# Rotating the second layer's queries and keys inside the projections, and summing the modulation with the ones as the stationary operand

## The reference

```python
mod_l = (silu(c) @ w_mod[l] + b_mod[l])
mod_c = (silu(c_ctx) @ w_mod[l] + b_mod[l])
```

```python
x1, x2 = x[..., :half], x[..., half:]
rotated = concatenate([x1 * cos - x2 * sin, x2 * cos + x1 * sin])
o = attend(qn, rotate(qr), kn, rotate(kr), v)
```

## Time and profile before

| | |
|---|---|
| Runs of the kernel before | 2794.28, 2802.24, 2805.22 us (median 2802.24) |
| The profiled execution | 2797.42 us, of which the span of its instructions is 2795.4 us |
| TensorE busy | 2476.6 us (89% of the span) |
| VectorE busy | 1182.4 us (42%) |
| ScalarE busy | 422.6 us (15%) |
| GpSimd busy | 856.1 us (31%) |
| Mean granted TensorE clock | 0.938 of full speed |

### The profile page before, as it was taken

The page is one execution under the profiler, slowest core; times in us unless marked ns, Lnnn a source line. Parts: engine busy times, 40 slices in busy tenths (PEclk is TensorE's granted clock), DMA queues, the critical chain, the costliest instruction groups (busy, mean ns, idle before and its releaser), DMA issues. The chain is left out here.

```text
span 2795.4 us, 30212 instructions
## 1 busy us (share of the span) xinstructions
PE 2476.6 (89%) x8861; PEld 1129.2 (40%) x8862; DVE 1182.4 (42%) x2415; ACT 422.6 (15%) x891; POOL 856.1 (31%) x1012
## 2 busy tenths in 40 slices
PE   6999887693799999999995997997399999999995
PEld 2565344441333333333332643554233333333332
DVE  2998364635523233332349213322632332323227
ACT  2000145020000000000013212322000000000002
POOL 0111102110454545545413001001255455454532
PEclk8999878796899999999997999998699999999997
DMA  6757001102699999999965300101589999999857
GB/s 247 231 196 241 20 1 61 51 30 84 242 368 368 354 353 355 356 365 359 365 260 223 94 31 9 61 23 41 202 310 345 337 330 338 336 335 335 332 209 278
DMA packets 164013, 634.28 MB, mean 227 GB/s; under 512 B 51710, under 2 KB 58282, under 8 KB 113634
## 3 DMA queue, kind: packets, MB, share of 16 engines
q10 hardware_dynamic: 59984, 389.57, 37.6%
q0 software_dynamic: 55280, 129.67, 12.8%
q1 hardware_dynamic: 48676, 114.13, 11.0%
HBM read 609.96 MB, written 74.58 MB: 245 GB/s over the span
## 5 line engine op out<-in xcount | busy, mean ns | idle before, releaser
L1813 POOL DMA_INDIRECT xg<-rows_x,p_idx x520 | 529.3, 1018 | 232.2 <-issue 124.6
L1901 PE MATMUL p_gu<-ring,p_xT 128*128 128x512 f32 x1024 | 455.8, 599 | 26.3 <-DVE p_xT L2142 26.3
L1913 PE MATMUL p_gu<-ring,p_xT 128*64 x1024 | 453.2, 595 | 0.0
L1914 PE MATMUL p_gu<-ring,p_xT 128*64 128x512 f32 x1024 | 453.1, 595 | 0.0
L2148 DVE TENSOR_TENSOR p_hid<-p_gu,p_sg 128x256 f32<-128x256 f32 x128 | 54.4, 425 | 580.6 <-ACT p_sg L2026 580.6
L1901 PEld LDWEIGHTS p_gu<-ring,p_xT 128*128 128x128 f32 x1024 | 192.0, 193 | 244.4 <-issue 244.4
L2142 DVE STREAM_TRANSPOSE p_xT<-xg 128x1024 f32<-128x1024 f32 x130 | 263.7, 2028 | 28.8 <-DMA xg<-rows_x,p_idx 27.1
L2158 DVE COPY p_ys<-p_y 128x512 f32<-128x512 f32 x128 | 88.5, 692 | 365.8 <-PE p_y L1942 187.8
L1913 PEld LDWEIGHTS p_gu<-ring,p_xT 128*64 128x64 f32 x1024 | 135.0, 137 | 263.9 <-issue 256.2
L1940 PE MATMUL p_y<-ring,p_hT 128*64 x512 | 233.4, 598 | 5.1 <-issue 5.1
L1929 PE MATMUL p_y<-ring,p_hT 128*128 128x512 f32 x512 | 236.8, 605 | 0.0
(11 more groups left out here) (450 smaller groups left out, 2975.7 us busy)
## 6 DMA issues: line engine op xcount, KB each, us to landing
ring<-in_w_exp_gate ACTq DMA_DIRECT2D x120, 1024.0 KB
ring<-in_w_exp_up ACTq DMA_DIRECT2D x120, 1024.0 KB
ring<-in_w_exp_down ACTq DMA_DIRECT2D x120, 1024.0 KB
ring<-rows_y SPq DMA_DIRECT2D x80, 512.0 KB, 13.0
decays<-in_w_mod POOLq DMA_DIRECT2D x24, 1024.0 KB
cat_e<-in_w_mod POOLq DMA_DIRECT2D x16, 1024.0 KB, 6.2
xg<-rows_x,p_idx POOLq DMA_INDIRECT x520
p_wmod<-in_w_mod SPq DMA_DIRECT2D x4, 2048.0 KB, 19.7
```

The costliest lines, as they stand in the source:

```text
L1813: nc.gpsimd.indirect_dma_start(out=xg[q][:, part * D // QUADS:(part + 1) * D // QUADS], out_offset=None, in_=tr.rows_x[:, :].rearrange("t ...
L1901: mm = nc.tensor.matmul(gu[q][:], xT[q][:, k, :], w[:, :, k, :], start=(k == 0), stop=(k == KD - 1))
L1913: nc.tensor.matmul(gu[q][lower, :], xT[q][:, k, lower], wa[:, :, k, :], start=first, stop=last)
L1914: mm = nc.tensor.matmul(gu[q][upper, :], xT[q][:, k, upper], wb[:, :, k, :], start=first, stop=last)
```

## The change

The rotation's phase goes. `latent_up` gets its work: the two loads on SyncE behind the load of `wk`, a tile's swap product on TensorE behind jobs 12, 17, 22, 27 and 32 (`krT` first), the product with the sines on VectorE one job later, the cosines on GpSimd, and the sum on VectorE ahead of jobs 16, 21, 26, 31 and 36. Two of the eight banks are given to the swap products.

In `even_project` the column of ones becomes the stationary operand and the item's buffer of 256 columns the moving one, so an item takes one matmul that writes one row of 256 numbers, at partition 0 or 64 of one of two banks. TensorE waits once, for the last item of the pair, and issues both products. ScalarE copies each row to SBUF, behind its drain of the job, and SyncE stores each row with a transfer of its own (64 in all, 1 KB each). The transpose and VectorE's two copies go.

```diff
@@ even_project
-        mcols, mturn = ph.ps("mcols", [P, P]), ph.ps("mturn", [P, P])
+        rows = spare[:, 4:6, :].rearrange("p t (a n) -> p (t a) n", n=MC)
+        sums = [ph.ps(f"sums{i}", [P, 512]) for i in range(2)]
             @block.sync
-                sp.wait_ge(mod_rows, 1)
-                for layer, s, ms in runs:
-                    r, lo = column[ms[0]], slices[items[ms[0]][0]][1] * MC
-                    sp.dma_start(tr.mod_raw[layer, s, lo:lo + len(ms) * MC].rearrange("(r c) -> r c", c=P),
-                                 mrows[r:r + HALVES * len(ms), :]).then_inc(stored, 16)
-                sp.wait_ge(stored, 16 * len(runs))
+                for m, (i, s) in enumerate(items):
+                    layer, n = slices[i]
+                    sp.wait_ge(copied, m + 1)
+                    sp.dma_start(tr.mod_raw[layer, s:s + 1, n * MC:(n + 1) * MC],
+                                 rows[m % 2 * SUB:m % 2 * SUB + 1, m // 2 % ROWS, :]).then_inc(stored[m // 2 % ROWS], 16)
+                for q in range(ROWS):
+                    sp.wait_ge(stored[q], 16 * sum(m // 2 % ROWS == q for m in range(len(items))))
             @block.tensor
                     for m in in_slot[n - 1] if n else []:
-                        pe.wait_ge(part_done, m + 1)
-                        for i in range(HALVES):
-                            mm = nc.tensor.matmul(mcols[:, column[m] + i:column[m] + i + 1],
-                                                  part[m % ABUF][:, i * P:(i + 1) * P], tr.ones[:, 0:1],
-                                                  start=True, stop=True)
-                        mm.then_inc(reduced, 1)
-                    if n == slots + 1:
-                        pe.wait_ge(copied, 1)
-                        nc.tensor.transpose(mturn[:], columns, tr.ident[:]).then_inc(mod_turned, 1)
+                        pe.wait_ge(part_done, in_slot[n - 1][-1] + 1)
+                        if m >= 4:
+                            pe.wait_ge(copied, m - 3)
+                        at = m % 2 * SUB
+                        nc.tensor.matmul(sums[m // 2 % 2][at:at + 1, 0:MC], tr.ones[:, 0:1], part[m % ABUF][:],
+                                         start=True, stop=True).then_inc(reduced, 1)
             @block.vector
-                    if n == slots + 1:
-                        dve.wait_ge(reduced, len(items))
-                        nc.vector.tensor_copy(columns, mcols[:]).then_inc(copied, 1)
-                        dve.wait_ge(mod_turned, 1)
-                        nc.vector.tensor_copy(mrows, mturn[:]).then_inc(mod_rows, 1)
             @block.scalar
+                    for m in in_slot[n - 1] if n else []:
+                        act.wait_ge(reduced, m + 1)
+                        q, at = m // 2 % ROWS, m % 2 * SUB
+                        if m >= 2 * ROWS:
+                            act.wait_ge(stored[q], 32 * (m // (2 * ROWS)))
+                        nc.scalar.copy(rows[at:at + 1, q, :], sums[m // 2 % 2][at:at + 1, 0:MC]).then_inc(copied, 1)
@@ latent_up
-    NB = 8
+    NB = 6
+    FIRST, APART = MH + MH // 2, 5
+    rotating = [krT[:, NCTX:T]] + [qrT[:, i, :] for i in range(MH // 2)]
             @block.sync
+                sp.dma_start(swap[:], dr["c_swap"]).then_inc(rope_loaded, 16)
+                sp.dma_start(rope[:], dr["c_rope"]).then_inc(rope_loaded, 16)
+            @block.gpsimd
+            def _(pool):
+                pool.wait_ge(rope_loaded, 32)
+                for n, x in enumerate(rotating):
+                    pool.wait_ge(swapped, n + 1)
+                    nc.gpsimd.tensor_tensor(x, x, rope[:, 0, :], ALU.mult).then_inc(cosines, 1)
             @block.tensor
+                def swap_halves(n):
+                    if n == 0:
+                        pe.wait_ge(rope_loaded, 32)
+                    else:
+                        at = jobs.index(("qr", n - 1, 0))
+                        pe.wait_ge(read_dve if engines[at] == "dve" else read_act, drains.count(at + 1, engines[at]))
+                    if n >= 2:
+                        pe.wait_ge(sines, n - 1)
+                    nc.tensor.matmul(swaps[n % 2][:], swap[:], rotating[n], start=True, stop=True).then_inc(swapped, 1)
...
+                    if n >= FIRST and (n - FIRST) % APART == 0 and (n - FIRST) // APART < len(rotating):
+                        swap_halves((n - FIRST) // APART)
             @block.vector
+                    if n > FIRST and (n - FIRST) % APART == 1 and (n - FIRST) // APART < len(rotating):
+                        turn_halves((n - FIRST) // APART)
+                    if n > FIRST and (n - FIRST) % APART == 4 and (n - FIRST) // APART < len(rotating):
+                        add_cosines((n - FIRST) // APART)
@@ odd_mixer
-                rotate(tr, [qrT[:, i, :] for i in range(MH // 2)] + [krT[:, NCTX:T]])
```

More of the change, by code:

```diff
@@ L375, in even_project @@
     in_slot = [[m for m in range(len(items)) if m // 2 * slots // (len(items) // 2) == n] for n in range(len(jobs))]
[L376 to L379, removed]
+    ROWS = 8
     loads = [1, 1, 1 + 2 * SKV + 1, 2, 1 + 2 * SKV + 1 + 1]
@@ L388, in even_project @@
         part = [ph.sb(f"part{i}", [P, MC]) for i in range(ABUF)]
-        columns, mrows = (spare[:, 4, i * P:(i + 1) * P] for i in range(2))
-        mcols, mturn = ph.ps("mcols", [P, P]), ph.ps("mturn", [P, P])
+        rows = spare[:, 4:6, :].rearrange("p t (a n) -> p (t a) n", n=MC)
+        sums = [ph.ps(f"sums{i}", [P, 512]) for i in range(2)]
         wm_loaded = [ph.sem(f"wm_loaded{i}") for i in range(MBUF)]
         term, part_done, reduced = ph.sem("term"), ph.sem("part_done"), ph.sem("reduced")
-        copied, mod_turned, mod_rows = ph.sem("mod_copied"), ph.sem("mod_turned"), ph.sem("mod_rows")
-        stored = ph.sem("mod_stored")
+        copied, stored = ph.sem("mod_copied"), [ph.sem(f"mod_stored{i}") for i in range(ROWS)]
         def target(kind, i, x):
@@ L717, in _ @@
                         .then_inc(gated, 1)
[L720 to L764, removed]
 def local_attention(tr, sqT, skT, sv, cat, qkT, aT, qa, kb, carry):
@@ L2401, in _, with latent_up @@
                 place(NT - 1)
-def latent_up(tr, cqT, ckvT, qnT, qrT, knT, v, wn, wr, q_loaded):
+def latent_up(tr, cqT, ckvT, qnT, qrT, knT, krT, v, wn, wr, q_loaded):
     nc, dr = tr.nc, tr.dram
@@ L2418, in latent_up @@
         bank = [ph.ps(f"bank{i}", [P, 512]) for i in range(NB)]
+        rope, swap, part = ph.sb("rope", [P, 2, NLAT]), ph.sb("swap", [P, P]), ph.sb("part", [P, 2, NLAT])
+        swaps = [ph.ps(f"swaps{i}", [P, NLAT]) for i in range(2)]
+        rope_loaded, swapped, sines = ph.sem("rope_loaded"), ph.sem("swapped"), ph.sem("sines")
+        cosines, rotated = ph.sem("cosines"), ph.sem("rotated")
         kv_loaded, product = ph.sem("kv_loaded"), ph.sem("product")
@@ L2459, in _, with turn_halves, add_cosines @@
                     mm.then_inc(product, 1)
+                    if n >= FIRST and (n - FIRST) % APART == 0 and (n - FIRST) // APART < len(rotating):
+                        swap_halves((n - FIRST) // APART)
             @block.vector
             def _(dve):
+                def turn_halves(n):
+                    dve.wait_ge(rope_loaded, 32)
+                    dve.wait_ge(swapped, n + 1)
+                    nc.vector.tensor_tensor(part[:, n % 2, :], swaps[n % 2][:], rope[:, 1, :], ALU.mult).then_inc(sines, 1)
+                def add_cosines(n):
+                    x = rotating[n]
+                    dve.wait_ge(sines, n + 1)
+                    dve.wait_ge(cosines, n + 1)
+                    nc.vector.tensor_tensor(x, x, part[:, n % 2, :], ALU.add).then_inc(rotated, 1)
                 for n, job in enumerate(jobs):
+                    if n > FIRST and (n - FIRST) % APART == 1 and (n - FIRST) // APART < len(rotating):
+                        turn_halves((n - FIRST) // APART)
+                    if n > FIRST and (n - FIRST) % APART == 4 and (n - FIRST) // APART < len(rotating):
+                        add_cosines((n - FIRST) // APART)
                     if engines[n] == "dve":
@@ L2713, in odd_mixer @@
                                     lambda sp: load_w_uq(sp, tr, wn, wr, uq_loaded))
-                    latent_up(tr, cqT, ckvT, qnT, qrT, knT, v, wn, wr, uq_loaded)
-                rotate(tr, [qrT[:, i, :] for i in range(MH // 2)] + [krT[:, NCTX:T]])
+                    latent_up(tr, cqT, ckvT, qnT, qrT, knT, krT, v, wn, wr, uq_loaded)
                 latent_attention(tr, qnT, qrT, knT, krT, v, cat, w[:].rearrange("p k n -> p (k n)"), lambda sp: sp.dma_start(
```

## The result

The changed kernel takes 2784.7 us (median of 7 runs, 2776.7 to 2786.2); the kernel before has a median of 2802.24 us over 7 runs. The ratio is 0.9928 with a 95% interval of 0.9905 to 0.9952: 0.7% faster. The middle of that is over the half per cent; the near end of the interval, 0.48%, is just under it. The profiled execution is the median one, with a span of 2782.9 us against 2795.4.

A forecast was written before the change was run, and what follows sets the result against it. TensorE was taken to bound `latent_up`, TensorE and VectorE in turn `even_project`, with the rotation a mostly idle phase between barriers. 13.9 + 0.4 = 14.3 us off the 2799.8 us average gave 2785.5 us, range 2777 to 2796.

The forecast's parts named there:

- The rotation: Between `latent_up` and the scores: 16.51 us removed, 4.3 and 0.35 added, 2.05 gained by the clock; 13.9 us less.
- the sums: In `even_project`: a pair's four records take 0.86 us instead of 0.92; with phase-end costs, 0.4 us less in all.
- The term for more semaphores: End of `latent_up`: clearing ten semaphores instead of five costs 0.35 us more.
- The opening: First eight score records after `latent_up`: full clock after a short gap, 2.05 us gained, nothing as the other end.
- Rival (a): The scores still open at the slow clock: 2.05 us less gain, 2787.5 us; chance 0.16.
- One of my signs: After `even_project`: the first layer's next phase begins within 1 us of 316.8.
- Rival (c): `even_project` sums: one-column products don't overlap, 0.42 us or more a record; 2803 to 2810 us, slower; chance 0.05.
- Rival (b): `even_project` short jobs: the new sums keep TensorE's clock up, 3.1 us more gain, 2782.4 us; chance 0.10.
- Rival (d): `latent_up`: VectorE's rotation sums wait for GpSimd and hold the drains, 6.5 us lost, 2792.0 us; chance 0.08.

The follow-up runs named there:

- the run with the rotation alone: Kernel before with only the rotation moved into `latent_up` and the old `even_project` kept: 2789.5 us, ratio 0.9955.
- the idle stretch: Changed kernel plus eleven dependent ScalarE copies behind the last drain of `latent_up`, leaving TensorE idle before the scores: 2790.1 us, one run.
- the other layout: Changed kernel with the 32 pairs in `even_project` moved mostly to the 384-column and long jobs, one among the short: 2772.5 us, ratio 0.9905.

## Why the prediction was right, and where its terms were off

**The time.** Forecast 2785.5 us, measured 2784.7, inside the range. That it hit to 0.8 us is partly luck. Two errors of opposite sign lie in it: the sums were worth more than I said, and the trace lost 7 us in a stage that I had no term for. And the base was a choice: I took 14.3 us from 2799.8, while the medians lie 17.5 us apart and the two traces' spans 12.5. On the sign over half a per cent I stood on the fence, with 0.51 for "same" and 0.45 for "faster"; it came out at 0.7%, with an interval that just reaches under the half.

**The rotation: the steps held.** The stretch went; the swap products cost 0.86 us each on TensorE (1664.77 to 1665.63) and lengthened the phase's work by 4.3; the sines, cosines and sums were hidden; two banks fewer cost nothing. I summed 13.9 us; the first two traces show 14.2 and the run with the rotation alone 14.3. The second traces of each show 12.9: 12.0 up to the scores, but only 0.9 in the attention stage, where the changed kernel met the slow clock one unit later (147.5 us and not 146.0). The term for more semaphores was mis-sized: 0.94 us from the last drain to the scores, against 0.89 for the old end, and not 0.35 more.

**The opening.** I took 2.05 us of gain with nothing as the other end. The eight records took 2.82 us in all seven traces with the short gap, against 4.90 to 5.25 before, and the idle stretch brings the slow opening back. Rival (a) fell as I wrote it. What I did not see is that the slow opening can come one unit later: in three of the seven traces, the second of the changed kernel among them, the next eight records took 4.41 to 4.52 us and not 2.85, and 1.6 of the 2 us were given back. The Trainium skill, "TensorE: Matmul & The Clock Gate", Part 1, had made me doubt the gain by its freely running monitor. The first opening shows nothing of that, the second unit agrees with it: 2.85 us in one trace of the changed kernel and 4.44 in the other.

**The sums: the sign was right by luck, the size was wrong.** I said 0.4 us; the two traces show 4.6, of which 1.0 us are the first long job at a friendlier place of the slow clock (8.24 us from 219.44 against 9.20 from 222.85). The failed step is "After, it is 4 records of 256 columns ... 0.86 us": I counted the records one behind the other. They cost 0.53 us in their row, because the two products write partitions 0 and 64 and run side by side; on the same rows they take 0.96. One of my signs failed with this step: the next phase began at 311.0, and not within 1 us of 316.8. The other side was off too: 0.92 us is a pair behind a wait, and in a row the old pair cost 0.81 us (136.31 to 137.12). Against 0.81 my own 0.86 would have made the new sums dearer than the old ones, as they are on the same rows (6.32 us against 6.05). From sum to sum a pair is 0.17 us cheaper (I had 0.06; the 0.28 us between 0.81 and 0.53 don't all arrive, as from the job behind to the next sum it is 5.35 us and not 5.24), and `even_project` 4.8 us shorter over 32 pairs where TensorE sets the pace nearly throughout; it is less in this kernel, where VectorE sets it for most of the first seven pairs and in the short jobs. The Trainium skill has this in "TensorE: Matmul & The Clock Gate", Part 3, on packing small products: the partition at which an output starts in PSUM (0, 32, 64 or 96) fixes the columns of the array that its product uses, and products in different tiles of the array run concurrently. The traces agree: 0.96 us to 0.53. I read the diff's `at = m % 2 * SUB` as a place to put results and not as a choice of columns.

**Rival (c)**, one-column products that don't overlap at 418 ns each, was wrong by far: even on the same rows four records cost 0.96 us, 0.24 each, and a lone product's length says nothing of a row of them. **Rival (b)**, the full clock through the short jobs, did not come with the change (mean clock 0.80 from 200 to 219.4, and 0.85 before) but with the other layout, where it and the waits together made up most of the 12.4 us. **Rival (d)** did not happen: no sum of VectorE waited for GpSimd.

**What I had no term for.** A stage of 157 us that nobody touched took 7 us more in the trace. I had argued that a shorter stage moves all behind it forward by as much. That holds for the work and not for the places of the slow clock.

## What to carry to other kernels

Products with a narrow stationary operand are worth placing so that their results go to different partition groups (0 and 64 were tried here); issued next to each other, two of them then cost little more than half (0.53 us against 0.96). When a stream of small work is spread over jobs, spread it by the time that each job takes, not by the count of jobs: here that took about 11 us more out of the stage, where the change itself had taken 4.6. And when two traces are compared, look at the granted clock of the untouched stages before believing a difference under half a per cent.

## What the runs showed of the hardware

The same instructions took 156.6 to 164.7 us in a stage with short pauses of TensorE; in the long form a stretch of 16 us ran at 1.2 GHz (granted clock 0.50) that ran at 2.4 GHz in the short form (1.00). A stretch can stay at the 1.2 GHz level although TensorE is busy all the time: 16.00 of 16.00 us from 430 to 446.

GpSimd's products with the cosines took 1.27 us inside `latent_up`, against 1.49 on average in the old phase, and VectorE's sums 0.68 us against 1.11. In the old phase the sums, which read two SBUF tensors, ran beside GpSimd's products, and the one that began at 1714.41 lasted 1.66 us; here none runs beside one. The sine product, which reads one operand from PSUM, ran beside GpSimd at 1665.9 and neither was slower (0.69 and 1.27 us). The Trainium skill, "GPSIMD Engine Reference", Specifications, says that GpSimd's SBUF interfaces are shared with VectorE, with contention against VectorE instructions of two SBUF inputs; these rows agree.
